# Norms by token halves next to the neighbouring products, roots from bits on VectorE, and the context's norm inside a feed-forward part

## The reference, cut to what matters

```python
def rmsnorm(x, g):
    return x * rsqrt(mean(x * x, -1) + EPS) * g

# first block: two layers
h = rmsnorm(x, norm_mix)
a_x, a_b, a_c, q, k, v, ..., m_q, gate_logits = split(h @ w_in)
y_a = a_b * causal_conv3(a_c * a_x)          # and three more branches: sparse attention, a gated
merged = sum(gates[n] * (y[n] @ w_lift[n]))  # recurrence (hgrn), attention over mem; mem_n = rmsnorm(mem)
x = x + merged @ w_out
hf = rmsnorm(x, norm_ffn)
gate, up = split(hf @ w_up)
x = x + (silu(gate) * up) @ w_down

# second block: modulate(x, ...) = rmsnorm(x, w) * (1 + scale) + shift
shift, scale, gate, ... = split(silu(c) @ mod_w[i] + mod_b[i])   # and the same from c_ctx for the context
a, ac = modulate(x, ...), modulate(ctx, ...)
h = h + g1 * mixer(a, ac)     # layer 0: gated delta rule and gated linear attention over context and
                              # latent tokens, products gk, gv, gq, lq, lk, lv, lg, gz; layer 1: hyena
h = h + g2 * swiglu(modulate(h, ...))
return rmsnorm(h, final_norm)
```

## Time and profile before

| | |
|---|---|
| median of 3 runs | 2562.18 us (2560.21 to 2562.65) |
| profiled execution, its own time | 2562.15 us |
| its span, first to last instruction | 2560.4 us |
| TensorE busy | 90% of the span |
| VectorE, ScalarE, GpSimd busy | 48%, 29%, 2% |
| mean granted TensorE clock | 0.934 of full speed |
| moved by DMA | 348.57 MB, 136 GB/s on average |

### The profile page before, as it was taken

The page is one execution under the profiler, slowest core; times in us unless marked ns, Lnnn a source line. Parts: engine busy times, 40 slices in busy tenths (PEclk is TensorE's granted clock), DMA queues, the critical chain, the costliest instruction groups (busy, mean ns, idle before and its releaser), DMA issues.

```text
span 2560.4 us, 32758 instructions
## 1 busy us (share of the span) xinstructions
PE 2306.1 (90%) x13870; PEld 1906.8 (74%) x13870; DVE 1236.7 (48%) x1990; ACT 743.9 (29%) x950; POOL 56.9 (2%) x78
## 2 busy tenths in 40 slices
PE   6999989899989998998998899897789979988996
PEld 5867768589978577785997776884469966645996
DVE  3331338588623314344886332667445534543543
ACT  3113430234311325203333332122334421003442
POOL 0000000000000000000000000000010000000000
PEclk9999989999989989899999899988689989999998
DMA  6333336577643324265786012000155523202551
GB/s 215 133 115 115 118 113 214 182 263 263 212 118 135 115 83 148 85 229 197 263 280 216 4 66 99 2 2 34 33 176 190 187 99 107 99 0 95 189 186 66
DMA packets 206647, 348.57 MB, mean 136 GB/s; under 512 B 19555, under 2 KB 110442, under 8 KB 206117
## 3 DMA queue, kind: packets, MB, share of 16 engines
q1 hardware_dynamic: 191632, 291.09, 33.7%
q0 software_dynamic: 14592, 55.31, 6.4%
q10 hardware_dynamic: 276, 0.08, 0.0%
HBM read 345.41 MB, written 1.05 MB: 135 GB/s over the span
## 4 chain that ended last, share of the span: by engine, by line
PE 75%; DVE 15%; ACT 6%; issue 3%; DMA 0%; SPq 0%; DVEq 0%; ACTq 0%
PE psum L366 50%; PE psum L689 21%; DVE ring_low L977 3%; DVE A L1368 3%; DVE G L1060 2%; PE psum L426 1%; ACT high_weights L970 1%; DVE wide_room L1060 1%; ACT A L746 1%; ACT xn L753 1%; PE psum L410 1%; ACT L760 1%; DVE tmp L1060 1%; DVE x L1060 1%; DVE xn L1030 1%
## 5 line engine op out<-in xcount | busy, mean ns | idle before, releaser
L366 PE MATMUL psum<-hT,ring 128*128 128x256 f32 (+1 forms) x2784 | 622.7, 385 | 1.4 <-ACT hT L776 1.4
L366 PEld LDWEIGHTS psum<-hT,ring 128*128 128x128 f32 (+1 forms) x2784 | 531.3, 192 | 81.5 <-issue 5.6
L977 DVE TENSOR_TENSOR ring_low<-ring,high_weights 128x2048 fp32r<-128x2048 f32 x132 | 302.6, 2292 | 227.0 <-ACT high_weights L970 225.0
L689 PE MATMUL psum<-high_rows,high_weights 128*128 128x256 f32 x1408 | 399.4, 284 | 12.7 <-DVE ring_low L977 10.1
L689 PE MATMUL psum<-high_rows,ring_low 128*128 128x256 f32 x1408 | 395.4, 281 | 0.0
L689 PE MATMUL psum<-hT_low,high_weights 128*128 128x256 f32 x1408 | 395.4, 281 | 0.0
L689 PEld LDWEIGHTS psum<-high_rows,high_weights 128*128 128x128 f32 x1408 | 266.8, 189 | 17.1 <-issue 13.2
L689 PEld LDWEIGHTS psum<-hT_low,high_weights 128*128 128x128 f32 x1408 | 266.7, 189 | 0.6
L970 ACT ACTIVATE high_weights<-ring 128x2048 fp32r<-128x2048 f32 x132 | 253.1, 1917 | 45.7 <-DMA ring<-in_ffn_w_up_dram 41.7
L689 PEld LDWEIGHTS psum<-high_rows,ring_low 128*128 128x128 f32 x1408 | 266.3, 189 | 0.0
L1368 DVE SCALAR_TENSOR_TENSOR A<-A,silu_c 128x256 f32<-128x256 f32 x392 | 190.1, 485 | 14.0
(11 more groups left out here) (414 smaller groups left out, 2524.7 us busy)
## 6 DMA issues: line engine op xcount, KB each, us to landing
ring<-in_w_in_dram SPq DMA_DIRECT2D x36, 2048.0 KB, 7.8
ring<-in_ffn_w_dram SPq DMA_DIRECT2D x66, 1024.0 KB, 5.3
A<-in_mod_w_dram POOLq DMA_DIRECT2D x48, 1024.0 KB, 7.8
ring<-in_ffn_w_up_dram SPq DMA_DIRECT2D x44, 1024.0 KB, 5.5
ring<-in_ffn_w_down_dram SPq DMA_DIRECT2D x22, 1024.0 KB, 5.9
ring<-in_w_lift_dram SPq DMA_DIRECT2D x16, 1024.0 KB, 8.7
ring<-in_ab_w_in_dram SPq DMA_DIRECT2D x7, 2048.0 KB, 8.0
ring<-in_hy_w_in_dram SPq DMA_DIRECT2D x6, 2048.0 KB, 7.9
```

What stands on the lines that cost most here:

```text
L366: return pe.eng.matmul(out, lhsT, rhs, start=(k == 0), stop=(k == n - 1))
L689: ins = pe.eng.matmul(out, lhs[a], rhs[b], start=first and n == 0, stop=last and n == 2)
L977: v.eng.tensor_tensor(low, whole, high.bitcast(F32), ALU.subtract).then_inc(*v.mark(f"w_lo/{l}.{i}"))
```

## The change

Every norm is cut by token halves. `norm_turned(key, t)` waits for one half and transposes it in eight products; evictions cover four feature pieces of one half. The products around it are put in an order in which half 0 is used while half 1 is still made:

- a_x (both layers), hy_in.0, and step 0 of all four ffn parts run in 128 columns: half 0's products first, half 1's transposes shortly before half 0's products end, then half 1's.
- In front of a ffn norm, TensorE transposes half 0 before the last product of the output projection, and VectorE scales half 0 before its last residual add.
- Step 9's down products leave their place between up 10 and down 10: after up 10 come down 9 and down 10 for half 0, then both for half 1, and each half is marked done by itself (`ffn_half`).
- The residual adds go half by half, next to the norm that follows.

The inverse root is taken on VectorE, from a first guess by shift and subtraction of the bits and three Newton steps; logarithm and exponential and their table loads go for all norms, the query roots, the hgrn roots and the heads' roots. The two big key roots (mk, gk) stay on ScalarE. The context's norm moves into the second ffn part: squares in step 5, scaling in step 6, transposes in steps 8 and 9, in rooms of their own. The gated layer begins with lv: its context products stand first, around the transposes of lat0. The gate rows (`spread`) of the second block's ffn parts come behind step 0. Input and result are moved in halves, and the context's load goes ahead of 15 of the modulation loads on GpSimd's queue.

```diff
+CTX_SQUARES, CTX_SCALED, CTX_TURNS = 5, 6, (8, 9)
...
         top["pe"] = dict(mm=mm, panel=panel, turn=turn)
...
-        def norm(key):
-
-            pe.wait_ge(*reached(f"xn/{key}.0"))
...
+        def norm_turned(key, t):
+
+            rows = rows_of.get(key, xn)
+            pe.wait_ge(*reached(f"xn/{key}.{t}"))
+            for g in range(2):
+                label = f"xnT_ready/{key}.{t}.{g}"
+                b = fixed(label, 4 + 2 * t + g) if key == "mem" else take(label)
+                for i in range(4):
+                    k = 4 * g + i
+                    ins = pe.eng.transpose(b[:, i * P:(i + 1) * P], rows[:, t, k * P:(k + 1) * P], ident[:, :])
                 ins.then_inc(*pe.mark(label))
 
...
+        def transposed_by_half(names, labels, key, w, used, read=None):
+
+            b = [take(label) for label in labels]
+            for t, tok in enumerate(TOKENS):
+                for u in range(2):
+                    for c in range(2):
+                        if (t, u, c) == (0, 1, 1):
+                            norm_turned(key, 1)
+                        for k in range(KD):
+                            if u == 0 and c == 0 and k % 4 == 0:
+                                pe.wait_ge(*reached(f"hT/{key}.{t}.{k // 4}"))
+                            ins = mm(b[u][:, c * SEQ + t * P:c * SEQ + (t + 1) * P],
+                                     w[:, k, (2 * u + c) * P:(2 * u + c + 1) * P], hT[:, k, tok], k, KD)
+                    if t:
+                        ins.then_inc(*pe.mark(labels[u], [used] if u else []))
...
+                        if (half, t, k) == (1, 1, KD - 1):
+                            norm_turned(f"ffn{l}", 0)
...
-            norm(f"ffn{l}")
-            ffn_tensor(l, f"hT/ffn{l}")
...
+                if j == 0:
+                    labels = [f"{('ffn_gate', 'ffn_up')[g]}_ready/{l}.0" for g in range(2)]
+                    b = [banks.take(label) for label in labels]
+                    for t, tok in enumerate(TOKENS):
+                        for g in range(2):
+                            w, used = panel(f"up{l}.0.{g}")
+                            wh, wl = parts(g)
+                            for c in range(2):
+                                if (t, g, c) == (0, 1, 1):
+                                    top["pe_norm"](key, 1)
+                                ins = up_product(b[g], c, tok, wh, wl, None if g or c else f"hT/{key}.{t}")
+                            if t:
+                                ins.then_inc(*pe.mark(labels[g], [used]))
+                    if l in top["gate_spread"]:
+                        top["gate_spread"][l]["pe"]()
...
+                if 0 < j < FFN_STEPS - 1:
                     i = j - 1
...
+                if j == FFN_STEPS:
+                    for t in range(MT):
+                        for i in (FFN_STEPS - 2, FFN_STEPS - 1):
+                            wh, wl, used = down_parts(i)
+                            ins = down_product(i, t, wh, wl)
+                            if t:
+                                ins.then_inc(*pe.mark(f"down_done/{l}.{i}", [used] + ([f"ffn_ready/{l}", f"ffn_half/{l}.1"] if i == FFN_STEPS - 1 else [])))
+                            elif i == FFN_STEPS - 1:
+                                ins.then_inc(*pe.mark(f"ffn_half/{l}.0"))
...
+                if l == 1 and j in CTX_TURNS:
+                    top["pe_norm"]("ctx", CTX_TURNS.index(j))
...
+                for i in range(4):
+                    k = 4 + i
+                    e.activation(dst[:, k, TOKENS[t]], b[:, i * P:(i + 1) * P], ACT.Identity, scale=gain[:, k:k + 1],
+                                 bias=shift[:, k:k + 1]).then_inc(
+                        *a.mark(f"{'raw_hT' if split else 'hT'}/{key}.{t}.1" if i == 3 else None, ["read " + label] if i == 3 else ()))
...
+            if j == 0 and l in top["gate_spread"]:
+                top["gate_spread"][l]["act"]()
+            if l == 1 and j == CTX_SQUARES:
+                for t in range(MT):
+                    top["act_squared"]("ctx", t, top["ctx_rows"], "ctx_in/0")
+            if l == 1 and j in CTX_TURNS:
+                top["act_norm"]("ctx", CTX_TURNS.index(j), top["gain"][:, 0, :], top["mod"][:, 0, 0:8, 1])
...
+        def stats(key, t):
+
+            s, half, y, tmp = (st[:, i + t:i + t + 1] for i in (0, 2, 4, 6))
+            v.wait_ge(*reached(f"sumsq/{key}.{t}"))
+            e.tensor_scalar(half, s, -0.5 / D, -0.5 * EPS, ALU.mult, ALU.add).then_inc(*v.mark(f"ms/{key}.{t}"))
+            v.wait_ge(*v.own())
+            e.tensor_scalar(y.bitcast(I32), half.bitcast(I32), 1, None, ALU.logical_shift_right).then_inc(*v.mark())
+            v.wait_ge(*v.own())
+            e.tensor_scalar(y.bitcast(I32), y.bitcast(I32), -1.0, float(0x5F3759DF + 0x40000000 - 0x400000), ALU.mult,
+                            ALU.add).then_inc(*v.mark())
+            v.wait_ge(*v.own())
+            for i in range(3):
+                e.tensor_scalar(tmp, y, y, half, ALU.mult, ALU.mult).then_inc(*v.mark())
+                v.wait_ge(*v.own())
+                e.scalar_tensor_tensor(y, tmp, 1.5, y, ALU.add, ALU.mult).then_inc(*v.mark())
+                v.wait_ge(*v.own())
+
+        def norm_rows(key, t, src):
+
+            stats(key, t)
+            e.tensor_scalar(rows_of.get(key, xn)[:, t, :], src[:, t, :], st[:, 4 + t:5 + t], None, ALU.mult).then_inc(*v.mark(f"xn/{key}.{t}"))
+            v.wait_ge(*v.own())
+
...
+                    tt(dst[:, 4 * g:4 * g + 4, TOKENS[t]], b.rearrange("p (k t) -> p k t", k=4),
+                       gain[:, 4 * g:4 * g + 4].unsqueeze(2).broadcast_to([P, 4, P]), ALU.mult, done, ["read " + label])
...
+                    for k in range(4):
+                        ts(dst[:, k, TOKENS[t]], b[:, k * P:(k + 1) * P], gain[:, k:k + 1], shift[:, k:k + 1], ALU.mult, ALU.add,
+                           done if k == 3 else None, ["read " + label] if k == 3 else ())
...
+        def ffn_residual(l, t):
+
+            v.wait_ge(*reached(f"ffn_half/{l}.{t}"))
+            b = B(f"ffn_ready/{l}")
+            for half in range(2):
+                r = x[:, t, half * HALF:(half + 1) * HALF]
+                tt(r, r, b[:, 2 * t + half, :], ALU.add, f"x/{l}.{2 * t + half}", [f"read ffn_ready/{l}"] if t and half else ())
...
+            for t in range(MT):
+                if l:
+                    ffn_residual(l - 1, t)
+                norm_rows(f"mix{l}", t, x)
+                if t == 0 and l:
+                    norm_out(f"mix{l}", 0, PA[:, 8 * l:8 * l + 8])
...
+            if l == 1 and j == CTX_SCALED:
+                for t in range(MT):
+                    top["dve"]["norm_rows"]("ctx", t, top["ctx_rows"])
+            if l == 1 and j in CTX_TURNS:
+                top["dve"]["norm_out"]("ctx", CTX_TURNS.index(j), top["gain"][:, 0, :], top["mod"][:, 0, 0:8, 1])
...
-    plan = ["gk", "gv", "gq", "small2", "lqk", "lv", "lg", "gz", "ab_out.0", "ab_out.1"]
+    plan = ["lv", "gk", "gv", "gq", "small2", "lqk", "lg", "gz", "ab_out.0", "ab_out.1"]
...
                     ins = mm(b, src[s][:, k, t * P:(t + 1) * P], w[:, k, :], k, KD)
                 ins.then_inc(*pe.mark(label, used if t else []))
+                if name == "lv" and s == 0:
+                    norm_turned("lat0", t)
...
+        w, used = panel("lv")
+        tokens("lv", w, [], 0, lambda t: hTs[0])
+        tokens("lv", w, [used], 1, lambda t: hTs[1][2 * t:2 * t + 2])
         w, used = panel("gk")
...
-        w, used = panel("lv")
-        tokens("lv", w, [], 0)
-        tokens("lv", w, [used], 1)
...
+                transposed(f"hy{i}", w, [used], 1)
 
...
+        def ffn_add(l, t):
+
+            v.wait_ge(*reached(f"ffn_half/{l}.{t}"))
+            b = bank_of(marks, psum, f"ffn_ready/{l}")
+            for half in range(2):
+                r, z = x[:, t, half * HALF:(half + 1) * HALF], b[:, 2 * t + half, :]
+                v.wait_ge(*reached(f"gate2_row/{l - 2}.{half}"))
+                tt(z, z, row[:, half * HALF:(half + 1) * HALF], ALU.mult)
...
@@ -2449,8 +2625,7 @@
             v.wait_ge(*reached(f"head_sq/{n}.1"))
...
-            v.wait_ge(*reached(f"head_rs0/{n}"))
-            newton(None, heads[:, 2, c], heads[:, 1, c], heads[:, 3, c])
+            root(heads[:, 2, c], heads[:, 1, c], heads[:, 3, c])
...
-        ts(st[:, 2:4], st[:, 0:2], 1.0 / D, EPS, ALU.mult, ALU.add, "ms/final")
-        v.wait_ge(*reached("rs0/final"))
...
         for t in range(MT):
+            ffn_add(3, t)
+            stats("final", t)
+            v.wait_ge(*reached("final_row/0"))
...
+            for t in range(MT):
+                sp.wait_ge(*reached(f"result/{t}"))
+                sp.eng.dma_start(out[0][t * P:(t + 1) * P, :], x[:, t, :]).then_inc(*sp.loads(f"stored_{t}/0"))
...
+                    if i == 24 + 9:
+                        pool.wait_ge(*reached("merged/1.3.3"))
```

(18 more changed lines are left out.)

389 lines of the change are left out of this document (205 added, 184 removed).

## The result

| | before | after |
|---|---|---|
| median | 2562.41 us (4 runs, 2560.21 to 2562.69) | 2599.53 us (4 runs, 2597.23 to 2605.93) |
| ratio | | 1.0151, 95% interval 1.0131 to 1.0171 |
| profiled span | 2560.4 us | 2604.1 us |

What follows compares the result with a forecast made beforehand. TensorE, busy for 90% of the span, bounds the kernel, so time is won only where it waits or its work shrinks. Terms 4.7+12+25.3+6.3+5.6-7.4-10.6 = 35.9 us, from 2562.15 to 2526; range 2495 to 2554.

Steps and rivals of the forecast that it cites:

- the price of step 0: Step 0 of each feed-forward part: 192 narrow products at 0.117 us, 22.5 us instead of 11.3, +11.2 in each of four.
- Rival A: Narrow rounded products in the four steps 0 run at f32's rate, 0.22 us each: 2605 us, chance 16%.
- if the first 24 take 5 us: Sign in the profile, at the start of step 0, that narrow rounded products run at f32's rate.
- The floor of the loads: On TensorE, loading 128x128 weights costs 0.115 to 0.119 us, taken as the least price of a narrow product.
- The start: Beginning of the program to the first branch: gain of 1 us, at norm mix0.
- Tails: End of each feed-forward part: TensorE waits for down 10's low weights, 2.6 us lost four times, 10.6 in sum.
- Norm mix1, lat1, final, heads, context with lv: Gains forecast: mix1 4.7, lat1 12, final norm 6.3, heads' roots 3.6, context and lat0 with lv moved 25.3 us.
- Rival C: Gated part: lv was cover after all, key norms stand open without it, 27 us come back: 2553 us, chance 6%.
- rival D: Norms: half 1's work queues behind half 0's, waits stay at 91 us; 2540 us, chance 4%.
- Ffn norms in halves: Norms ahead of the four feed-forward parts: -3.5, -3.3, 0 and -0.6, a loss of 7.4 us in sum.
- The cover for the context's norm: Second feed-forward part: its VectorE work fits beside one 4 us modulation per step; uncovered it would cost 8 us.

Runs made afterwards that it cites:

- e1: Changed kernel with step 0 of every feed-forward part in full width (256 columns), half 1 transposed ahead of it; 2544.0 us, ratio 0.9942.
- e3: Changed kernel with each of step 0's 192 products streaming 256 columns, same order of halves and as many weight loads; 2551.2 us, ratio 0.997.
- e4: Changed kernel with ScalarE evicting a_x ahead of the rotary tables and constants in the first layer; 2596.9 us, ratio 1.0146.
- e5: Changed kernel with step 0 in full width and a_x evicted ahead of the constants; 2533.0 us, ratio 0.9896.
- e7: As e5, but lv back behind lk and lat0's norm open at the start of the second block; 2549.4 us, ratio 0.9957.
- e8: As e5, but half 0 of the four feed-forward norms transposed behind the last output product and modulation, both halves squared before evicting; 2525.2 us, ratio 0.9866.
- e11: Plain f32 a_x (both layers) and hy_in.0 in full width, against a kernel combining all edits that paid; 2536.0 us, ratio 0.9893.
- e2: Kernel before the change, with gate and up products of step 5 of each feed-forward part in 128-column halves; 2614.8 us, ratio 1.0217.
- e12: Kernel before the change, with steps 3, 5 and 7 of each feed-forward part in 128-column halves; 2701.4 us, ratio 1.0546.
- e6: As e5, with step 9's down products back between up 10 and down 10, down 10 alone by halves; 2523.7 us, ratio 0.9857.

## Why the prediction was wrong, step by step

- **The failed step** is the price of step 0, "I take 0.117, nearest to the floor": the price at full clock was right (0.111), and what failed is that I carried it through the whole step as a constant. I had the earlier trace rows in hand, where the transposes behind such a wait run "at half clock", and priced the first ffn norm with them, but not what stands next. In the trace before, the clock came back over the plain f32 work directly ahead of step 0, the 16 transposes above all; the change puts half 0's eight ahead of the last output product, so that step 0 itself stands behind the wait for its low parts (1.04, 1.13, 2.89 and 2.89 us), with the clock at half within 3 us of its start, and its narrow products don't bring it back. A wide step 0 in the same place does (e1, e3). Step 0 with half 1's transposes took 41.0, 28.8, 39.4 and 40.8 us, 150.0 in all, where I had 23.5 each, 94: this is 56 of the 68.6 us missed in the feed-forward parts (86.6 against 18.0).
- **Rival A** named the place, the direction and, by chance, the size (2605). Its mechanism was another, and its sign in the profile too: "if the first 24 take 5 us"; the first 16 took 1.8 us. What should have stood beside it is the price of the step at half clock, a rival that I did not write down.
- **The floor of the loads** scales with the clock: at half clock a narrow and a wide rounded product both cost 0.213. The Trainium skill, "TensorE: Matmul & The Clock Gate", section "LDWEIGHTS (loading the stationary operand)", gives P / 1.2 ns for P columns, which by estimate is 107 ns for 128: near 0.111 at full clock, but half of what the rows show at half clock. The 81 ns that its section "Back-to-back issue gap" gives for 128 columns is below the 0.111 us that the rounded products took here at full clock.
- **The start** was forecast at +1 and lost 12.8: the table of who takes which bank was not followed through the new order. 8.8 are shown by e4 and e5, 1.7 are a_x's first weights, which land at 25.3, and the rest is half clock behind the wait.
- **Tails**: forecast 2.6 each; from up 10 to the last down product the four parts took 4.3, 4.2, 4.4 and 4.1 us more than before. In the last part the wait was as forecast, and the half clock behind it was left out. These are 6 more of the 68.6 us. Another 6 in these parts stay unassigned.
- **Norm mix1, lat1, final, heads, context with lv**: within 3.1 us each. Rival C is excluded by e7, rival D by the waits for scaled rows (17.9 us, where it has 91).
- **Ffn norms in halves**: forecast at a loss of 7.4 us, step 0's price included; e8 shows that half 0 ahead of the last product costs 2 us in each when step 0 is wide. With a narrow one this wasn't tried.
- The cover for the context's norm inside the second part held: no wait stands there.

## What to carry to other kernels

Price both halves before splitting a product to overlap it with what it waits for. In plain f32 a record of 256 columns took twice one of 128, so the split was free, and it hid the norm (e11). In the rounded type 256 columns took 0.117 us and 128 took 0.111, so the split doubled the step: 10 us more at full clock, some 30 at half. After a wait, put wide products first, as in e1 and e3, and price what stands behind a wait at half clock until the rows show it rising. When an order is changed, follow the rotation of buffers too, and ask who reads the one that comes next.

## What the runs showed of the hardware

- A stream of rounded products of 128 columns is busy in the record from end to end, and yet did not bring TensorE's clock back from 1.2 GHz (25.5 us at 0.50 above), nor take it down from 2.4 where no wait stood in it (21 us at 1.00 in e2). The Trainium skill ("TensorE: Matmul & The Clock Gate", section "What's actually happening") has it that activity releases the throttle; here the clock rose beside 256 columns and the same loads (e3), and beside 128 it did not.
- Eight plain f32 transposes among the narrow products (1.93 us at half clock) were followed by the rise in three of the four parts of the changed kernel, and not in the first.
- A fall followed a wait of only 0.70 and 0.64 us among narrow products (changed kernel); with 256 columns at the same places it did not (0.73 and 0.74 us, e3). It followed one of 1.01 us with one-column products ahead of it (e12), and in the next part the same sequence left the clock at full.
- The kernels scatter from one execution to the next: by 19 us in e2 and 21 in e4, which have narrow rounded steps, but without them still by 10 in the kernel before (2557.3 to 2567.1), 13 in e6 and e11, and by 3 in e1. One profile shows only one of these times.
